# A mixture-of-experts loop on one core: one code for the first block of every expert, and a short branch that takes a second block over the same weights

## The chip, the cores and the metric

The kernel runs on one core of a Trainium2 chip. The metric is the device time of one execution in microseconds (us). The chip, the inputs and the reference are the same before and after the change. The core's engines each follow a program of their own: TensorE (PE) multiplies, VectorE (DVE) and ScalarE (ACT) do element-wise work, SyncE (SP) issues the transfers. They meet at semaphores.

## The reference, cut to what matters

Two transformer blocks over 256 tokens of width 1024. The first has a recurrent branch, an attention and a feed-forward part; the second has two attentions and a mixture of 32 experts. The change is in the experts alone:

```python
logits = (xf @ w_router + b_router).astype(jnp.float32)
top_val, top_idx = lax.top_k(logits, TOP_K)            # 4 of 32 experts for each token
gates = jax.nn.softmax(top_val, axis=-1)
...
hid = xb @ w_mlp1[e] + b_mlp1[e]                       # 1024 -> 2048
glu = jnp.minimum(hid[..., ::2], SWIGLU_LIMIT)
lin = jnp.clip(hid[..., 1::2], -SWIGLU_LIMIT, SWIGLU_LIMIT)
act = glu * jax.nn.sigmoid(SWIGLU_ALPHA * glu) * (lin + 1.0)
return act @ w_mlp2[e] + b_mlp2[e]                     # 1024 -> 1024
```

256 tokens with 4 experts each give 1024 assignments, 32 for an expert on the mean. Everything is float32. Each expert's weights are 12 MB: 8 MB for the first product (the up stage) and 4 MB for the second (the down stage).

## The kernel before, in words

The program first runs the two blocks' dense parts, written out straight. Then comes one loop over the 32 experts, written out for each position `x` from 0 to 32, inside a `While` that repeats only when an expert has more than 128 tokens (here it runs once).

**Positions.** VectorE ranks the experts by their counts. Positions 0 and 1 keep experts 0 and 1; the others are filled from the ranking, the fullest at positions 13, 19, 7, 25 and so on. The rank table is known at run time only, so SP reads the expert number of a position from `order` before it loads its weights.

**Blocks.** A block is 64 tokens of an expert (`CAP`). Every expert computes one block. An expert with more than 64 tokens (`many[x]`, read by `crowded`) computes a second block with the same weights. In this data two experts do, at positions 13 and 19.

**Weights.** SP streams them from HBM into `ring`, 17 slots of 1 MB. An expert has 12 pieces of 1 MB: 8 of the up stage, 4 of the down stage. Piece `i` may be written when piece `i - 17` has been used, which TensorE tells by `m_piece`. In the list of pieces the up pieces of position `x + 1` stand ahead of the down pieces of `x`. The first 17 of the 384 pieces are loaded before the loop starts; the other 367 are issued inside it.

**One turn of the loop on TensorE**, at position `x`: the branch on `many[x]` (L962); the up stage `up(x, blocks)` (L898 adds the bias, L909 multiplies by the weights), written twice, once for both blocks and once for the first alone; the gather of the tokens of `x + 1` (L829); at every other position `add_pair` (L944), which adds the results of two experts to the output; the branch on `many[x - 1]` (L991) around the down stage `down(x - 1, blocks, m)` (L924), again written twice, with the transposes `turns(x)` (L845, L840) among it; then `gates(x + 1)` (L835) and the branch of `second_block(x + 1)` (L866), which gathers the tokens of a second block. The untaken code lies in the program all the same: the branch jumps over it.

**The other engines.** VectorE clips and multiplies the hidden values (L2064 to L2073 for the first block, L2084 to L2093 for the second), ScalarE computes the sigmoid and copies transposed tiles back. Where an expert has no second block, each engine's `Else` raises the semaphores (`n_...`) that the second block would have raised.

Of the kernel before, what the change touches and what calls it, by code (L numbers as in the profile page):

```python
# [15 lines left out]
S = 256  # L16
# [99 lines left out]
zer f_sq f_acc f_tr  # L116
# [6 lines left out]
m_at m_aT m_ypa m_ypv m_pair m_left m_rank m_rank_v m_perm m_order  # L123
n_vec n_sel n_gath n_xg n_selt n_selT n_xet n_xe n_glu n_hid n_sig n_actd n_at n_aT n_y n_out
# [17 lines left out]
class Board:  # L142
# [244 lines left out]

    def up_at(self, x):

        return 12 * x - 4 if x else 0  # L390
# [20 lines left out]
def sync_program(e, K):  # L411
# [64 lines left out]
def tensor_program(e, K):  # L476
# [329 lines left out]
    e.wait_ge(S.zer, 1)  # L806
# [74 lines left out]
    def up(x, blocks):  # L881
        if x:
            e.wait_ge(S.m_aT, x)
            e.wait_ge(S.n_aT, x)
            e.wait_ge(S.n_y, x - 1)
        for c in blocks:
            if c:
                e.wait_ge(S.n_xe, x + 1)
                e.wait_ge(S.n_selT, x + 1)
            if c and x >= 2:  # L890
                e.wait_ge(S.m_ypa, x - 1)
                e.wait_ge(S.m_ypv, x - 1)
            if c and x == 0:
                e.wait_ge(S.m_order, 1)
            for n in range(2):
                for hf in range(2):
                    o0 = hf * 1024 + n * 512
                    mm(HID[c][n][64 * hf:64 * hf + 64, :], K.sel96[:, x:x + 1].to_broadcast([96, 64]),  # L898
                       K.b1h[:, o0:o0 + 512], start=True, stop=False, skip_group_check=True)
        for k in range(8):  # L900
            v = expert_piece(K.up_at(x) + k)
            if k == 0:
                e.wait_ge(S.m_xe, x + 1)
            xo = 128 * (k % 4) + 64 * (k // 4)
            for c in blocks:
                for n in range(2):
                    for hf in range(2):
                        o0 = hf * 1024 + n * 512
                        ins = mm(HID[c][n][64 * hf:64 * hf + 64, :], K.xe[c][x % 2][:, xo:xo + 64], v[:, o0:o0 + 512],  # L909
                                 start=False, stop=(k == 7), skip_group_check=True)  # L910
                        if k == 7 and c == n == 0 and hf == 1:
                            ins.then_inc(S.m_up0, 1)
            ins.then_inc(S.m_piece, 1)

    def down(x, blocks, m):

        v = expert_piece(K.down_at(x) + m)
        for j in range(2):
            kt = 2 * m + j
            q, hf = kt % 4, kt // 4  # L920
            for c in blocks:
                for oh in range(2):
                    g = 64 * (oh if c else oh ^ x % 2)
                    ins = mm(B[1 if c else 2][g:g + 64, :], K.aT[c][x % 2][:, 128 * q + 64 * hf:128 * q + 64 * hf + 64],  # L924
                             v[:, j * 1024 + oh * 512:j * 1024 + oh * 512 + 512], start=(kt == 0), stop=(kt == 7),
                             skip_group_check=True)
        ins.then_inc(S.m_piece, 1)
# [20 lines left out]
    with e.While(lambda: rest_of(e, K) > 0):  # L948
# [11 lines left out]
        for x in range(NE + 1):  # L960
            if x < NE:
                with e.If(many[x]):  # L962
                    up(x, (0, 1))
# [4 lines left out]
                with e.Else():  # L968
                    up(x, (0,))
# [12 lines left out]
            else:  # L982
# [5 lines left out]
                if x >= 2:  # L988
                    e.wait_ge(S.m_ypa, x - 1)
                    e.wait_ge(S.m_ypv, x - 1)  # L990
                with e.If(many[x - 1]):  # L991
                    turns(x)
                    e.wait_ge(S.n_aT, min(x + 1, NE))
                    e.wait_ge(S.m_hid, min(2 * x + 2, 2 * NE))
                    for m in range(4):
                        down(x - 1, (0, 1), m)
                    e.wait_ge(S.n_y, x)
                    e.wait_ge(S.n_selT, x)
                    for tt in range(2):
                        for oh in range(2):  # L1000
                            ins = mm(OUT[tt][oh][:, :],  # L1001
                                     K.selT[(x - 1) % 2][64 * oh:64 * oh + 64, tt * 128:(tt + 1) * 128],
                                     K.ysb[64 * oh:64 * oh + 64, :], start=False, stop=False, skip_group_check=True)
                    ins.then_inc(S.n_out, 1)
# [29 lines left out]
def scalar_program(e, K):  # L1034
# [296 lines left out]
    def second_block(x):  # L1331
        with e.If(many[x]):
            e.wait_ge(S.n_gath, x + 1)
            act(K.xg, B[3][:, :], ACT.Copy).then_inc(S.n_xg, 1)
            e.wait_ge(S.n_xet, x + 1)
            act(K.xe[1][x % 2], B[3][:, :], ACT.Copy).then_inc(S.n_xe, 1)
# [6 lines left out]
    def activate(x):  # L1343
# [7 lines left out]
        with e.If(many[x]):  # L1351
# [6 lines left out]
            if x >= 2:  # L1358
                e.wait_ge(S.m_piece, K.down_at(x - 2) + 4)
# [8 lines left out]
    with e.While(lambda: rest_of(e, K) > 0):  # L1368
# [4 lines left out]
        for x in range(NE + 1):  # L1373
# [12 lines left out]
            if x:  # L1386
                with e.If(many[x - 1]):
                    e.wait_ge(S.m_piece, K.down_at(x - 1) + 4)
# [33 lines left out]
def vector_program(e, K):  # L1422
# [499 lines left out]
    e.memset(K.zeros, 0.0).then_inc(S.zer, 1)  # L1922
# [51 lines left out]
    def ranks():  # L1974
# [3 lines left out]
        stt(key, K.cntf[0:96], 32.0, tie, ALU.mult, ALU.add).then_inc(S.m_rank_v, 1)  # L1978
        e.wait_ge(S.m_rank_v, 1)
        tt_(hit, key, rep, ALU.mult).then_inc(S.m_rank_v, 1)  # L1980
        e.wait_ge(S.m_rank_v, 2)
        e.tensor_reduce(K.rk[:, 0:1], hit, AX.X, ALU.add).then_inc(S.m_rank_v, 1)
        e.wait_ge(S.m_rank_v, 3)
        ts_(above, key, K.rk[:, 0:1], None, ALU.is_gt).then_inc(S.m_rank_v, 1)
        e.wait_ge(S.m_rank_v, 4)
        e.tensor_reduce(K.rk[:, 1:2], above, AX.X, ALU.add).then_inc(S.m_rank_v, 1)
        e.wait_ge(S.m_rank_v, 5)
# [4 lines left out]
    def in_order():  # L1992
# [3 lines left out]
        e.tensor_copy(K.order[:, 64:96], B[2][0:1, 128:160]).then_inc(S.m_rank_v, 1)  # L1996
        e.wait_ge(S.m_rank_v, 6)
# [29 lines left out]
    def second_block(x):  # L2027
# [47 lines left out]
    def second_activate(x):  # L2075
        w = K.actb[1]
        with e.If(many[x]):
# [16 lines left out]
        with e.Else():  # L2094
            if x:
                e.wait_ge(S.n_actd, 2 * x)
            e.sem_inc(S.n_glu, 2)
# [4 lines left out]
    with e.While(lambda: rest_of(e, K) > 0):  # L2102
# [31 lines left out]
        e.wait_ge(S.m_left, 1)  # L2134
# [4 lines left out]
        e.wait_ge(S.m_left, 2)  # L2139
# [113 lines left out]
```

## Time and profile before

| | us |
|---|---|
| median of three runs | 1862.34 (1857.36 to 1863.3) |
| the profiled execution, its own time | 1857.66 |
| span of its profile, first to last instruction | 1855.9 |
| TensorE busy in the span | 1674.7 (90%) |
| TensorE's weight loads | 927.6 (50%) |
| VectorE busy | 534.5 (29%) |
| ScalarE busy | 332.4 (18%) |

The profiled execution takes 1.8 us more than its span. The expert loop begins on TensorE at about 801 us and its last matmul ends at 1832 us of the span (1828.36 + 3.67); what follows (a last norm, a transpose back and the store) takes 24 us. TensorE's busy time is the union of matmuls that overlap in pairs: the two halves of its columns work side by side. Idle time that is marked "issue" is time in which the engine waited for nothing that the profile shows: no semaphore came late in it.

### The profile page before, as it was taken

To read this page: it belongs to the slowest core of one execution; us is meant where nothing else is said; L and a number is where in the kernel's file an instruction comes from. 1 tells how busy PE (TensorE), PEld (TensorE's weight loads), DVE (VectorE), ACT (ScalarE), POOL (GpSimd) and SP (SyncE) were. 2 spreads that over 40 slices of the span, in tenths; PEclk is the share of its full clock that TensorE was granted. 3 is DMA by queue.
4 is the path that set the end of the run, shared out by engine and by line. 5 is a ranking of instruction groups with operands and counts; after the bars stand their busy time and mean duration, and the time that the engine had idled before them with its cause. 6 is when DMAs were issued, how large, how long until landed. Compare 5 with 4: busy or idle time off the path is not lost. (4 is left out here: it accounts for less than half of the span.)

```text
span 1855.9 us, 20731 instructions
## 1 busy us (share of the span) xinstructions
PE 1674.7 (90%) x7662; PEld 927.6 (50%) x7662; DVE 534.5 (29%) x1309; ACT 332.4 (18%) x604; POOL 0.2 (0%) x4
## 2 busy tenths in 40 slices
PE   5999898999999888788799997989998879999785
PEld 3888776888588765533233332323333323433232
DVE  2655421766200375321111211111121111121111
ACT  2135652121100133210101110000110000111002
POOL 0000000000000000000000000000000000000000
PEclk9999999999999898979899998989998999999897
DMA  9744358335895230349999999979998789999990
GB/s 390 317 159 167 128 183 329 122 136 202 324 421 186 95 114 8 109 186 398 400 372 415 415 416 415 417 311 348 416 415 341 311 321 368 415 415 416 415 399 29
DMA packets 93340, 544.99 MB, mean 294 GB/s; under 512 B 8912, under 2 KB 9424, under 8 KB 44016
## 3 DMA queue, kind: packets, MB, share of 16 engines
q1 hardware_dynamic: 92144, 540.87, 73.1%
q8 instruction: 122, 2.00, 0.4%
q10 hardware_dynamic: 1024, 1.71, 0.3%
q14 instruction: 50, 0.41, 0.1%
HBM read 541.50 MB, written 1.05 MB: 292 GB/s over the span
## 5 line engine op out<-in xcount | busy, mean ns | idle before, releaser
L909 PE MATMUL bank<-ring,scr 128*64 128x512 f32 x2176 | 503.8, 621 | 11.4 <-issue 11.4
L491 PE MATMUL bank<-hT,ring 128*128 128x256 f32 x1856 | 414.0, 384 | 9.6 <-ACT hT L1057 7.3
L491 PEld LDWEIGHTS bank<-hT,ring 128*128 128x128 f32 x1856 | 356.4, 193 | 64.8 <-issue 13.8
L909 PEld LDWEIGHTS bank<-ring,scr 128*64 128x64 f32 x2176 | 175.3, 144 | 325.0 <-issue 321.3
L924 PE MATMUL bank<-ring,hT 128*64 128x512 f32 x1024 | 235.4, 597 | 1.3 <-DVE hT L2128 1.3
L2064 DVE TENSOR_SCALAR scr<-bank 128x256 f32<-128x256 f32 x64 | 27.0, 422 | 493.8 <-PE bank L909 493.8
L924 PEld LDWEIGHTS bank<-ring,hT 128*64 128x64 f32 x1024 | 71.7, 137 | 135.7 <-issue 135.7
L1350 ACT ACTIVATE scr<-scr 128x256 f32<-128x256 f32 x64 | 26.7, 417 | 600.1 <-DVE scr L2064 600.1
L2128 DVE COPY hT<-bank 64x512 f32<-64x512 f32 x32 | 22.2, 694 | 316.9 <-PE bank L924 316.9
L650 PE MATMUL bank<-scr,ring 128*128 128x256 f32 x384 | 83.4, 379 | 0.1
L829 PE MATMUL bank<-scr 128*64 128x512 f32 x272 | 73.1, 648 | 6.6 <-DVE scr L2036 4.6
L650 PEld LDWEIGHTS bank<-scr,ring 128*128 128x128 f32 x384 | 72.9, 190 | 10.2 <-issue 0.3
L898 PE MATMUL bank<-scr 96*64 96x512 bf16 x136 | 26.3, 474 | 52.1 <-issue 51.4
L944 PE MATMUL bank<-hT,scr 128*128 128x512 f32 x128 | 60.4, 616 | 0.8 <-ACT hT L1399 0.8
L1383 ACT ACTIVATE hT<-bank 128x512 f32<-128x512 f32 x32 | 19.1, 597 | 212.6 <-PE bank L845 212.6
L829 PEld LDWEIGHTS bank<-scr 128*64 128x64 f32 x272 | 21.7, 146 | 47.0 <-issue 39.1
L510 PE MATMUL bank<-ring,crep 128*32 128x512 f32 x384 | 42.7, 594 | 0.8 <-DMA ring<-in_w_ada 0.8
L944 PEld LDWEIGHTS bank<-hT,scr 128*128 128x128 f32 x128 | 23.7, 195 | 39.0 <-issue 37.3
L845 PEld LDWEIGHTS bank<-con,scr 128*128 128x128 f32 x136 | 15.1, 147 | 40.7 <-issue 25.0
L898 PEld LDWEIGHTS bank<-scr 96*64 96x64 bf16 x136 | 5.7, 116 | 58.9 <-issue 58.9
L499 PE MATMUL bank<-scr,con 128*128 128x256 f32 x40 | 14.8, 457 | 22.3 <-ACT scr L1078 16.3
L845 PE MATMUL bank<-con,scr 128*128 128x128 f32 x136 | 23.7, 300 | 12.1 <-DVE scr L2093 10.6
(369 smaller groups left out, 1273.4 us busy)
## 6 DMA issues: line engine op xcount, KB each, us to landing
ring<-in_w_mlp SPq DMA_DIRECT2D x384, 1024.0 KB, 14.0
ring<-in_w_in SPq DMA_DIRECT2D x28, 1024.0 KB, 25.6
ring<-in_ada_w SPq DMA_DIRECT2D x24, 1024.0 KB, 4.9
ring<-in_up SPq DMA_DIRECT2D x24, 1024.0 KB, 12.3
ring<-in_w_ada SPq DMA_DIRECT2D x24, 1024.0 KB, 9.0
ring<-in_down SPq DMA_DIRECT2D x12, 1024.0 KB, 25.9
ring<-in_w2in SPq DMA_DIRECT2D x6, 1024.0 KB, 26.9
ring<-in_w_out SPq DMA_DIRECT2D x4, 1024.0 KB, 5.8
```

The source lines that it names most:

```text
L491: ins = mm(b[:, 256 * j:256 * j + 256], v[:, k * 256 + j * 128:k * 256 + j * 128 + 128], rhs[:, k, :], start=(k == 0), stop=(k == 7))
L510: ins = mm(B[5][32 * j:32 * j + 32, :], K.crep[:, k, :], v[:, 512 * j:512 * j + 512], start=(k == 0), stop=(k == 7))
L650: ins = mm(b[j][:, 0:256], v[:, k * 256 + j * 128:k * 256 + j * 128 + 128], K.ff[:, kk * 8 + k, :], start=(kk == 0 and k == 0), stop=(kk = ...
L829: ins = mm(B[3][64 * hf:64 * hf + 64, :], K.sel[c][:, tt, :], K.h4[:, tt, hf * 512:(hf + 1) * 512], start=(tt == 0), stop=(tt == 1), skip_ ...
L845: ins = e.transpose(B[c][:, 128 * q:128 * q + 128], K.actb[c][:, 128 * q:128 * q + 128], ident)
L898: mm(HID[c][n][64 * hf:64 * hf + 64, :], K.sel96[:, x:x + 1].to_broadcast([96, 64]), K.b1h[:, o0:o0 + 512], start=True, stop=False, skip_g ...
L909: ins = mm(HID[c][n][64 * hf:64 * hf + 64, :], K.xe[c][x % 2][:, xo:xo + 64], v[:, o0:o0 + 512], start=False, stop=(k == 7), skip_group_ch ...
L924: ins = mm(B[1 if c else 2][g:g + 64, :], K.aT[c][x % 2][:, 128 * q + 64 * hf:128 * q + 64 * hf + 64], v[:, j * 1024 + oh * 512:j * 1024 + ...
L944: ins = mm(OUT[tt][oh][:, :], K.pairT[p % 2][oh][:, tt * 128:(tt + 1) * 128], K.ypair[oh], start=False, stop=False, skip_group_check=True)
L1350: act(K.w2[:, sl], K.actb[0][:, sl], ACT.Sigmoid, scale=1.702).then_inc(S.m_sig, 1)
L2064: ts_(w[:, sl], gate, 7.0, None, ALU.min).then_inc(S.m_glu, 1)
L2128: e.tensor_copy(K.ypair[1 - (x - 1) % 2][64:128, :], B[2][64:128, :]).then_inc(S.m_ypv, 1)
```

## The change

The second block gets code of its own, on TensorE alone:

- `up(x)` now computes the first block of every expert and stands ahead of the branch. The branch on `many[x]` then holds `second_up(x)`, which passes over the same 8 pieces again.
- In the down stage the pieces of the first block (`down(x - 1, m)`), with `turns(x)` ahead of the last one as it was for uncrowded experts, stand ahead of the branch. The branch holds `second_down(x - 1)`, which passes over the same 4 pieces again and adds the second block to the output.
- `m_piece` is now raised when the first block has used a piece. Two new semaphores, `n_up` and `n_down`, count the second uses. Before SP overwrites a piece it waits for both. Where there is no second block, VectorE's `Else` raises `n_up` by 8 (in `second_block`) and `n_down` by 4 (in `second_activate`).
- The waits of ScalarE and VectorE that meant "both blocks have used this" now name `n_up` or `n_down`. Three semaphores are folded into others (`zer` into `consts`, `m_rank_v` into `m_left`), with the same waits.

```diff
+    def second_use(self, i):
+
+        if i < 8:
+            return self.S.n_up, i + 1
+        x, n = (i - 8) // 12, (i - 8) % 12
+        if x < NE - 1 and n < 8:
+            return self.S.n_up, 8 * (x + 1) + n + 1
+        return (self.S.n_down, 4 * x + n - 7) if x < NE - 1 else (self.S.n_down, 4 * x + n + 1)
...
             e.wait_ge(S.m_piece, i - RING + 1)
+            second, value = K.second_use(i - RING)
+            e.wait_ge(second, value)
             src = K.moe_source(i, expert[x])
...
+    def second_up(x):
+
+        e.wait_ge(S.n_xe, x + 1)
+        e.wait_ge(S.n_selT, x + 1)
+        if x >= 2:
+            e.wait_ge(S.m_ypa, x - 1)
+            e.wait_ge(S.m_ypv, x - 1)
+        if x == 0:
+            e.wait_ge(S.m_order, 1)
+        up_bias(x, 1)
+        for k in range(8):
+            v = expert_piece(K.up_at(x) + k)
+            xo = 128 * (k % 4) + 64 * (k // 4)
+            for n in range(2):
+                for hf in range(2):
+                    o0 = hf * 1024 + n * 512
+                    ins = mm(HID[1][n][64 * hf:64 * hf + 64, :], K.xe[1][x % 2][:, xo:xo + 64], v[:, o0:o0 + 512],
+                             start=False, stop=(k == 7), skip_group_check=True)
+            ins.then_inc(S.n_up, 1)
...
+    def second_down(x):
+
+        e.wait_ge(S.n_aT, min(x + 2, NE))
+        e.wait_ge(S.m_hid, min(2 * x + 4, 2 * NE))
+        for m in range(4):
+            down_piece(x, 1, m).then_inc(S.n_down, 1)
+        e.wait_ge(S.n_y, x + 1)
+        e.wait_ge(S.n_selT, x + 1)
...
             if x < NE:
+                up(x)
                 with e.If(many[x]):
-                    up(x, (0, 1))
+                    second_up(x)
                     e.wait_ge(S.n_actd, 2 * x + 2)
                     e.wait_ge(S.n_hid, 2 * x + 2)
                     e.wait_ge(S.m_hid, 2 * x + 2)
                     turn_hidden(1).then_inc(S.n_at, 1)
                 with e.Else():
-                    up(x, (0,))
                     if x:
                         e.wait_ge(S.n_at, x)
                     e.sem_inc(S.n_at, 1)
...
+                for m in range(3):
+                    down(x - 1, m)
+                turns(x)
+                down(x - 1, 3)
                 with e.If(many[x - 1]):
-                    turns(x)
-                    e.wait_ge(S.n_aT, min(x + 1, NE))
-                    e.wait_ge(S.m_hid, min(2 * x + 2, 2 * NE))
-                    for m in range(4):
-                        down(x - 1, (0, 1), m)
...
+                    second_down(x - 1)
                 with e.Else():
-                    for m in range(3):
-                        down(x - 1, (0,), m)
-                    turns(x)
-                    down(x - 1, (0,), 3)
...
             if x:
                 e.wait_ge(S.n_selT, x)
+                e.wait_ge(S.n_up, 8 * x)
+            e.sem_inc(S.n_up, 8)
...
-                e.wait_ge(S.m_piece, K.up_at(x) + 8)
+                e.wait_ge(S.n_up, 8 * x + 8)
...
             if x:
                 e.wait_ge(S.n_actd, 2 * x)
+                e.wait_ge(S.n_down, 4 * x)
+            e.sem_inc(S.n_down, 4)
```

**The up stage in TensorE's program.** In the program before, this stands at each position from `x = 2` on, where a turn of the loop begins (one row may be several matmuls, `x64` for instance; a float32 matmul of these rows becomes two records of a matmul and two of a weight load in the profile, a bfloat16 one or a transpose one of each):

```order
L962 COMPARE_AND_BRANCH
L898 MATMUL bank<-scr 64x512 x8
L909 MATMUL bank<-ring,scr 64x512 x64
L845 MATMUL bank<-con,scr 128x128 x4
L962 UNCONDITIONAL_BRANCH
L898 MATMUL bank<-scr 64x512 x4
L909 MATMUL bank<-ring,scr 64x512 x32
L968 UNCONDITIONAL_BRANCH
L829 MATMUL bank<-scr 64x512 x4
```

In the changed program the same place reads:

```order
L896 MATMUL bank<-scr 64x512 x4
L913 MATMUL bank<-ring,scr 64x512 x32
L1003 COMPARE_AND_BRANCH
L896 MATMUL bank<-scr 64x512 x4
L935 MATMUL bank<-ring,scr 64x512 x32
L856 MATMUL bank<-con,scr 128x128 x4
L1003 UNCONDITIONAL_BRANCH
L1009 UNCONDITIONAL_BRANCH
L840 MATMUL bank<-scr 64x512 x4
```

The branch has moved from ahead of the up stage to behind it, and it now skips one pass of 32 weight matmuls where it skipped 64.

**The down stage in TensorE's program.** Before, the end of the skipped code, the code for one block, and what follows it:

```order
L1001 MATMUL bank<-scr 128x512 x4
L991 UNCONDITIONAL_BRANCH
L924 MATMUL bank<-ring,hT 64x512 x12
L845 MATMUL bank<-con,scr 128x128 x4
L840 MATMUL bank<-con,scr 128x128 x4
L924 MATMUL bank<-ring,hT 64x512 x4
L1005 UNCONDITIONAL_BRANCH
L835 MATMUL bank<-con,scr 128x128 x2
L866 COMPARE_AND_BRANCH
```

In the changed program, from the first down piece on:

```order
L946 MATMUL bank<-ring,hT 64x512 x12
L856 MATMUL bank<-con,scr 128x128 x4
L851 MATMUL bank<-con,scr 128x128 x4
L946 MATMUL bank<-ring,hT 64x512 x4
L1035 COMPARE_AND_BRANCH
L946 MATMUL bank<-ring,scr 64x512 x16
L965 MATMUL bank<-scr 128x512 x4
L1035 UNCONDITIONAL_BRANCH
L1037 UNCONDITIONAL_BRANCH
L846 MATMUL bank<-con,scr 128x128 x2
L877 COMPARE_AND_BRANCH
```

The branch of the down stage now comes behind the last piece and skips 16 weight matmuls and 4 that add to the output; two branches (L1035 and L877) stand close together ahead of the next up stage.

## Rows read from the trace of the kernel before

**Rows 1.** The page: span; GB/s in 40 slices of the span.
```profile
span 1855.9 us, 20731 instructions
GB/s 390 317 159 167 128 183 329 122 136 202 324 421 186 95 114 8 109 186 398 400 372 415 415 416 415 417 311 348 416 415 341 311 321 368 415 415 416 415 399 29
```

**Rows 2.** The chain that ended last, positions 26 to 28: start, us, what.
```profile
1641.16 0.55 PE bank L898 x4
1641.71 13.73 PE bank L909 x64
...
1665.57 0.55 PE bank L898 x4
...
1693.77 0.55 PE bank L898 x4
```

**Rows 3.** SP's transfers from 806 us; two stretches: PEclk, DMA share, GB/s last.
```profile
806.51 42.60 SPq L444 DMA_DIRECT2D ring<-in_w_mlp  x17
829.00:834.00 5.00, 5.00 (x18) 1.80 (x16) 0.93 (x4) 0.00 (x0) 0.00 (x0) 0.58 0.02 7
1600.00:1700.00 100.00, 100.00 (x466) 36.80 (x464) 21.66 (x60) 12.43 (x24) 0.00 (x0) 1.00 1.02 415
```

**Rows 4.** TensorE's waits, positions 2 to 30: us in total, times, longest.
```profile
PE bank L898 <- issue: 50.6, 10, 5.5
PE bank L909 <- issue: 6.4, 3, 2.6
```

**Rows 5.** TensorE's timeline at positions 11, 20 and 29; idle ahead in brackets.
```profile
1120.22 1.07 PE L898 MATMUL bank<-scr 96*64 96x512 bf16 x4 [4.66 <-issue]
...
1453.61 1.06 PE L898 MATMUL bank<-scr 96*64 96x512 bf16 x4 [4.69 <-issue]
...
1723.33 1.06 PE L898 MATMUL bank<-scr 96*64 96x512 bf16 x4 [5.14 <-issue]
```

**Rows 6.** The chain that ended last, positions 22 and 23.
```profile
1524.75 5.47 issue
...
1531.29 16.29 PE bank L909 x64
...
1561.26 1.90 issue
```

**Rows 7.** TensorE's timeline at the loop's end.
```profile
1791.95 15.80 PE L909 MATMUL bank<-ring,scr 128*64 128x512 f32 x64 [4.98 <-issue]
...
1825.63 1.89 PE L924 MATMUL bank<-ring,hT 128*64 128x512 f32 x8
...
1828.36 3.67 PE L944 MATMUL bank<-hT,scr 128*128 128x512 f32 x8 [0.84 <-ACT hT L1399]
```

**Rows 8.** The page's third part: packets, MB, share of the program queue.
```profile
q8 instruction: 122, 2.00, 0.4%
```

**Rows 9.** TensorE in stretches, the ten up stages behind waits: clock third from last.
```profile
1530.20:1547.40 17.20, 17.18 (x69) 0.82 0.73 282
...
sum 165.50, PE 165.27; mean PE 16.53
```

**Rows 10.** The page's groups: count, busy, mean ns, idle before them and its releaser.
```profile
L909 PE MATMUL bank<-ring,scr 128*64 128x512 f32 x2176 | 503.8, 621 | 11.4 <-issue 11.4
L924 PE MATMUL bank<-ring,hT 128*64 128x512 f32 x1024 | 235.4, 597 | 1.3 <-DVE hT L2128 1.3
```

**Rows 11.** Timelines of positions 13 (first row) and 19, on TensorE and VectorE.
```profile
1190.98 1.47 PE L898 MATMUL bank<-scr 96*64 96x512 bf16 x8
...
1397.10 28.99 PE L909 MATMUL bank<-ring,scr 128*64 128x512 f32 x128
1431.38 0.90 PE L845 MATMUL bank<-con,scr 128*128 128x128 f32 x3 [5.29 <-DVE scr L2093]
...
1428.17 0.42 DVE L2084 TENSOR_SCALAR scr<-bank 128x256 f32<-128x256 f32 x1
...
1430.57 0.75 DVE L2093 TENSOR_TENSOR scr<-scr 128x256 f32<-128x256 f32 x2
```

More of the change, by code:

```diff
@@ L879, in second_block, with up_bias, up @@
             e.sem_inc(S.n_selt, 1)
-    def up(x, blocks):
+    def up_bias(x, c):
+        for n in range(2):
+            for hf in range(2):
+                o0 = hf * 1024 + n * 512
+                mm(HID[c][n][64 * hf:64 * hf + 64, :], K.sel96[:, x:x + 1].to_broadcast([96, 64]),
+                   K.b1h[:, o0:o0 + 512], start=True, stop=False, skip_group_check=True)
+    def up(x):
         if x:
@@ L885, in up @@
             e.wait_ge(S.n_y, x - 1)
[L886 to L899, printed above, removed]
+        up_bias(x, 0)
         for k in range(8):
@@ L904, in up, with down_piece @@
             xo = 128 * (k % 4) + 64 * (k // 4)
[L905 to L912, printed above, removed]
-            ins.then_inc(S.m_piece, 1)
-    def down(x, blocks, m):
+            for n in range(2):
+                for hf in range(2):
+                    o0 = hf * 1024 + n * 512
+                    ins = mm(HID[0][n][64 * hf:64 * hf + 64, :], K.xe[0][x % 2][:, xo:xo + 64], v[:, o0:o0 + 512],
+                             start=False, stop=(k == 7), skip_group_check=True)
+                    if k == 7 and n == 0 and hf == 1:
+                        ins.then_inc(S.m_up0, 1)
+            ins.then_inc(S.m_piece, 1)
+    def second_up(x):
[10 more added lines that the diff above has]
+            xo = 128 * (k % 4) + 64 * (k // 4)
+            for n in range(2):
+                for hf in range(2):
+                    o0 = hf * 1024 + n * 512
+                    ins = mm(HID[1][n][64 * hf:64 * hf + 64, :], K.xe[1][x % 2][:, xo:xo + 64], v[:, o0:o0 + 512],
+                             start=False, stop=(k == 7), skip_group_check=True)
+            ins.then_inc(S.n_up, 1)
+    def down_piece(x, c, m):
         v = expert_piece(K.down_at(x) + m)
@@ L920, in down @@
             q, hf = kt % 4, kt // 4
[L921 to L927, printed above, removed]
+            for oh in range(2):
+                g = 64 * (oh if c else oh ^ x % 2)
+                ins = mm(B[1 if c else 2][g:g + 64, :], K.aT[c][x % 2][:, 128 * q + 64 * hf:128 * q + 64 * hf + 64],
+                         v[:, j * 1024 + oh * 512:j * 1024 + oh * 512 + 512], start=(kt == 0), stop=(kt == 7),
+                         skip_group_check=True)
+        return ins
+    def down(x, m):
+        down_piece(x, 0, m).then_inc(S.m_piece, 1)
+    def second_down(x):
[5 more added lines that the diff above has]
+        e.wait_ge(S.n_selT, x + 1)
+        for tt in range(2):
+            for oh in range(2):
+                ins = mm(OUT[tt][oh][:, :], K.selT[x % 2][64 * oh:64 * oh + 64, tt * 128:(tt + 1) * 128],
+                         K.ysb[64 * oh:64 * oh + 64, :], start=False, stop=False, skip_group_check=True)
+        ins.then_inc(S.n_out, 1)
     def turns(x):
@@ L1977, in ranks @@
         rep, tie, at = K.rankc[:, 0:32], K.rankc[:, 32:64], K.rankc[:, 64:96]
[L1978 to L1987, printed above, removed]
+        stt(key, K.cntf[0:96], 32.0, tie, ALU.mult, ALU.add).then_inc(S.m_left, 1)
+        e.wait_ge(S.m_left, 1)
+        tt_(hit, key, rep, ALU.mult).then_inc(S.m_left, 1)
+        e.wait_ge(S.m_left, 2)
+        e.tensor_reduce(K.rk[:, 0:1], hit, AX.X, ALU.add).then_inc(S.m_left, 1)
+        e.wait_ge(S.m_left, 3)
+        ts_(above, key, K.rk[:, 0:1], None, ALU.is_gt).then_inc(S.m_left, 1)
+        e.wait_ge(S.m_left, 4)
+        e.tensor_reduce(K.rk[:, 1:2], above, AX.X, ALU.add).then_inc(S.m_left, 1)
+        e.wait_ge(S.m_left, 5)
         ts_(K.sel96, at, K.rk[:, 1:2], None, ALU.is_equal)
@@ L1995, in in_order @@
         e.tensor_copy(K.gpx.rearrange("p a b -> p (a b)"), B[2][:, 0:128])
-        e.tensor_copy(K.order[:, 64:96], B[2][0:1, 128:160]).then_inc(S.m_rank_v, 1)
-        e.wait_ge(S.m_rank_v, 6)
+        e.tensor_copy(K.order[:, 64:96], B[2][0:1, 128:160]).then_inc(S.m_left, 1)
+        e.wait_ge(S.m_left, 6)
         e.tensor_single_scalar(K.order[:, 0:32], K.order[:, 64:96], 31, ALU.bitwise_and)
```

28 lines of the change are left out of this document (11 added, 17 removed).

## The prediction

> **What bounds the kernel now.** I read the page first, then the chain that ended last, then TensorE's waits and timeline. More than half of the span is the expert loop, from 801 to 1832 us. The page's slices of it show 415 GB/s in many places, and 311 to 372 in seven [rows 1].
>
> Two things run against each other there. TensorE needs 24.4 and 28.2 us for two quiet positions (from the bias at 1641.16 to the next at 1665.57, and on to 1693.77 [rows 2]), 26.3 on the mean. The weights of a position are 12 pieces of 1.049 MB; at the 415 GB/s of a full stretch [rows 3] a piece takes 2.53 us and a position 30.3. So the loads are the slower of the two and should never stop. They do stop: TensorE falls behind somewhere, and its ring of 17 fills.
>
> The waits tell where. Ahead of the bias of an up stage (L898) TensorE is idle ten times, 50.6 us in all, with no semaphore late [rows 4]. Counted along the timeline, it is at positions 2, 3, 4, then 11, 12, then 20, 21, 22, then 29, 30; the rows show 11, 20 and 29 [rows 5]. Three positions wait a shorter time inside the up stage (6.4 us in all [rows 4], as the 1.90 at 1561 [rows 6]), and the last position 4.98 [rows 7]. The pattern has a period of nine positions, whatever the data. What else repeats with the position is the program: each turn has about the same number of instructions, so after nine turns it stands again at the same phase of the unit in which the program is fetched. And the place is always right behind the branch of L962, which jumps over the code for two blocks. I therefore read these waits as TensorE's code: the jump's target hasn't been fetched. Code comes in pieces of 2.00 MB / 122 = 16.4 KB [rows 8].
>
> Behind each full wait the granted clock is low for a while: 0.82 of full speed over the up stage of position 22 [rows 9], which is full speed (2.4 GHz) and some us at the lower level (1.2); TensorE had been idle 5.47 us before [rows 6]. The ten up stages take 165.5 us from bias to gather [rows 9]; an undisturbed one takes 0.55 + 13.73 = 14.28 [rows 2]. The low clock costs 165.5 - 142.8 = 22.7 us.
>
> **The code that is skipped.** The order rows give 64 weight matmuls in the code that L962 jumps over. The count of records (2176 for 34 blocks of 32 matmuls [rows 10]) says two matmul records each, and as many weight loads: 256 instructions. With 8 bias matmuls and 4 transposes at 2 each it is 280, and some 287 with waits and branches. After the change it is 128 + 8 + 8 and the like, some 149. In the down stage it was 32 weight matmuls, 4 that add up and 8 transposes, some 164 instructions; now it is 16 and 4, some 84. The price of shorter skips stands in the trace: L991 passes over its 164 instructions 30 times, and the down stage's matmuls never wait for issue, only 1.3 us for VectorE [rows 10]. So 164 is free, 287 costs about 5 us in a third of its cases, and 149 and 84 lie below the free one. I take zero for both; the bound from the other side is that 149 costs in proportion to its length, half of today's waits.
>
> The Trainium skill ("Runtime: NRT & Kernel Launch", "Instruction fetch mechanics") says that code is refilled in blocks of 16 KiB, 256 instructions, strictly in sequence, and that a taken branch to a target outside the current two blocks stalls. The trace agrees with the block's size. By that rule a skip of 287 can pass a whole block and one of 149 or 84 can't: the zero above. But the same section gives TensorE room for 2048 instructions; by that figure a skip of 287 would hardly miss, the waits would be something else, and the time would be that of the no-change rival below.
>
> **The sum on TensorE.**
> - Ten waits ahead of the bias: -50.6.
> - Four shorter ones: -6.4 - 4.98 = -11.4. I take them as the same fetch seen later: the jump landed near the end of a unit, and the next was still coming.
> - The low clock behind the ten: -22.7. Behind the last position's wait: 15.80 [rows 7] less some 13.9 (the chain's 13.73 [rows 2] and the last record's tail), -1.9.
> - Positions 13 and 19. The up stage has the same matmuls, 128 records in 28.99 us [rows 11]. Then TensorE waited 5.29 us for VectorE, whose chain for the second block ran from 1428.17 to 1431.32, 3.15 us, behind the first block's. Now the first block's lies beside the 14 us of the second pass, and 3.3 us remain: -2.0 each, -4.0.
> - The branches at their new places. The one on `many[x]` (L1003) now comes behind 32 weight matmuls that TensorE still works off: 0. L1035 stands behind the last down piece, with L877 shortly behind; before, L866 and L962 stood there: 0. The bound above is 0.1 us in each of 32 turns, 3 us.
> - SP's added waits are on counts that VectorE raises well before; at one piece in 2.53 us nothing is late behind them: 0.
>
> That is -90.6, and TensorE would end its loop at 1832.0 - 90.6 = 1741.4.
>
> **The sum on the loads.** The first of the 367 is issued at 806.51 [rows 3], when position 0 has used a piece; nothing can be earlier, as the ring is full until then. Near 829 to 834 us nothing moves (7 GB/s [rows 3]), in a part before any of the waits: +4.4. Then 367 x 2.527 = 927.3. The last piece lands at about 806.5 + 4.4 + 927.3 + 2 (my estimate for the way of one piece) = 1740.2. Behind it lie its eight matmuls 1.89, 0.84 for copying and the last pair 3.67 [rows 7]: 6.4. The loop can't end before 1746.6.
>
> **Which is last.** Position 13 starts at 1190.98 [rows 11]; half of 50.6 + 22.7 and a short wait of 2 fall away ahead of it, so TensorE is there at about 1152. Its first piece is the 136th of the loop's loads: 806.5 + 4.4 + 343.7 + 2 = 1156.6. The 17 pieces of lead are used up by then and TensorE waits some 5 us; the second block then gives the loads their lead back. TensorE's sum becomes 1746, beside 1746.6. Two limits that meet cost a little more than either; I take 1748, 84 us earlier than now. What follows the loop is untouched. The profiled execution's own 1857.66 becomes 1773.6, and 1775 with half of the branches' bound. The median of the runs shown, 1862.3, is 4.7 above the profiled one; I add one: **1776**.
>
> What is late next is the load stream: at positions 9 to 12 and at the end TensorE should stand idle for pieces.
>
> **The rivals.**
> - *Half of the waits stay*, because 149 misses in proportion: five waits of 5.06 + 2.27, 37 us, so 1813. Against it: 164 never missed.
> - *The ring is held.* At positions 13 and 19 eight pieces stay for a second pass of 14.3 us and four for 7.2. If all loads stopped that long, 2 x 21.5 = 43 us: 1819. Against it: 17 - 8 = 9 slots hold 22.7 us of loads, more than 14.3, as long as TensorE isn't many pieces behind when it comes there; by the sum it is ahead. I take 0, the bound is 43.
> - *No change.* The idle isn't code but a semaphore raised late by an `Else`, which the profile doesn't name. Then only -4.0: 1854. Against it: the period of nine.
> - *Slower.* It is not the length but two jumps in a row that make code late: today's ten waits stand behind L866 and L962, and L1035 and L877 are such a pair in every turn. A wait costs 5.06 + 2.27 = 7.3 us; from 90.6 / 7.3 = 12.4 such positions on the kernel is slower, at 30 it is at 1857.7 - 90.6 + 219 = 1986. Against it: the same pair passes twenty positions without a wait today, and the new pair skips only 115 instructions together.
> - *The clock.* Starved of pieces, TensorE may be granted the lower level where it wasn't; an up piece then takes 3.43 instead of 13.73 / 8 = 1.72 us, more than its load. If that happens in a third of some 60 starved us the loop loses about ten: 1786. It widens the range.
>
> **How the numbers follow.** Forecast 0.72, at 1766 to 1795; half stays 0.12; ring held 0.05; no change 0.04; slower 0.03; other mixtures between, 0.04. The range 1764 to 1806 holds the forecast with its bounds (clock, branches, load rate) and the lower part of the second case: 8 in 10. Faster by over 0.3% (about what a measurement of this kernel can tell from no change) 0.94, within 0.3% 0.03, slower 0.03.
>
> **What the profile after would show.** Right: no issue wait ahead of the bias (L896); under 100 packets in the program's queue; slices of the loop near 415 GB/s except the first; TensorE idle ahead of the up stage's weight matmuls (L913), short and often, at positions 9 to 12 and the end; 3.3 us of waiting at 13 and 19. Wrong: waits of about 5 us behind L1003 or L877 at every n-th position (code is still late), or none and yet under 400 GB/s around positions 13 and 19 (the ring is held). With the mechanism right, the load rate would make the number wrong: one per cent of it is 9 us.

## The result, and the profile after

The changed kernel takes 1789.03 us (median of four, 1787.89 to 1797.2) beside 1861.86 of the kernel before on the same chip: 0.962 of its time, 95% interval 0.960 to 0.965. The forecast was 1776, with a range of 1764 to 1806. A second timing of the same kernel (`again`, below) gave the same ratio, 0.962. The profiled execution was the slowest of the four, at 1797.2.

The page of the changed kernel:

```profile
span 1795.4 us, 21192 instructions
...
GB/s 394 336 141 174 131 131 392 109 120 220 218 422 312 115 120 47 71 50 327 417 415 417 416 417 416 416 417 413 415 415 362 367 379 418 415 418 414 418 415 123
...
q8 instruction: 95, 1.56, 0.4%
...
L913 PE MATMUL bank<-ring,scr 128*64 128x512 f32 x2048 | 458.4, 599 | 20.3 <-DMA ring<-in_w_mlp 20.0
...
L946 PE MATMUL bank<-ring,hT 128*64 128x512 f32 x1024 | 234.1, 597 | 4.4 <-DMA ring<-in_w_mlp 3.3
```

Of the seven slices of the loop that had stood at 311 to 372 GB/s [rows 1], three are left, 362, 367 and 379. The program queue moves 95 packets for 122 [rows 8]. TensorE's waits in the loop (us in total, times, longest):

```profile
PE bank L913 <- DMA ring<-in_w_mlp: 20.0, 36, 1.4
PE bank L856 <- DVE scr L2125: 6.7, 2, 3.4
PE bank L840 <- DVE scr L2066: 4.6, 2, 2.3
PE bank L946 <- DMA ring<-in_w_mlp: 3.3, 6, 0.6
...
PE bank L896 <- issue: 0.2, 1, 0.2
```

The 50.6 us ahead of the bias [rows 4] are 0.2. In their place TensorE waits 36 times ahead of the up stage's weight matmuls and 6 times ahead of the down stage's, all for pieces, 23.3 us. L856 are the transposes of the second block's hidden values at the crowded positions 13 and 19: 3.35 us of waiting each where it had been 5.29 [rows 11].

The records of the branches themselves, on TensorE's sequencer, show what the waits only suggest. Columns: count, duration of one in ns (shortest, median, longest). The kernel before:

```profile
L962 PEldq COMPARE_BRANCH  x34: 70/345/6071, 802.0 to 1785.6; - x34
L991 PEldq COMPARE_BRANCH  x34: 70/333/4421, 843.2 to 1820.0; - x34
```

and after:

```profile
L1003 PEldq COMPARE_BRANCH  x34: 70/208/346, 818.7 to 1744.2; - x34
L1035 PEldq COMPARE_BRANCH  x34: 70/210/369, 854.8 to 1764.5; - x34
```

In the kernel before, L962 takes 5.2 to 6.1 us at exactly the ten positions of the waits, and under 0.6 at all others; afterwards no branch takes over 0.4. The row of L991 also corrects a reading of mine: one of its 34 did take 4.42 us (at 1228, in the turn of position 13), behind matmuls that TensorE had still to work off, so that no wait was to be seen. A skip of 164 was nearly free, not free. That one record stands 1.2 us behind another jump: TensorE had just left the code for two blocks and passed over the up stage for one.

What is left is in the loads. The timeline of position 19, and stretches around it and behind it (granted clock third from last, GB/s last):

```profile
1369.50 1.06 PE L896 MATMUL bank<-scr 96*64 96x512 bf16 x4
1370.35 15.86 PE L913 MATMUL bank<-ring,scr 128*64 128x512 f32 x64
1386.04 0.60 PE L896 MATMUL bank<-scr 96*64 96x512 bf16 x4
1386.48 13.90 PE L935 MATMUL bank<-ring,scr 128*64 128x512 f32 x64
```
```profile
1370.00:1380.00 10.00, 10.00 (x40) 3.12 (x38) 0.86 (x5) 0.00 (x0) 0.00 (x0) 0.79 1.02 421
1380.00:1384.00 4.00, 4.00 (x22) 1.34 (x20) 0.00 (x0) 0.00 (x0) 0.00 (x0) 1.00 0.73 307
1384.00:1388.00 4.00, 4.00 (x24) 1.36 (x22) 2.29 (x7) 0.83 (x2) 0.00 (x0) 1.00 0.31 127
1388.00:1392.00 4.00, 4.00 (x20) 1.24 (x18) 0.66 (x2) 0.00 (x0) 0.00 (x0) 1.00 0.54 197
...
1412.00:1425.00 13.00, 13.00 (x68) 4.75 (x66) 2.47 (x7) 1.68 (x3) 0.00 (x0) 1.00 0.78 297
```
```profile
1346.00:1481.00 135.00, 127.28 (x566) 43.30 (x564) 23.39 (x66) 14.96 (x29) 0.00 (x0) 0.95 0.92 369
1482.00:1650.00 168.00, 168.00 (x784) 57.84 (x785) 34.93 (x97) 19.21 (x37) 0.00 (x0) 1.00 1.02 416
```

While the first pass (L913) runs, SP may not overwrite any of the eight pieces: it issues nothing between 1366.3 and 1388.6, the seven pieces that are on their way when the pass begins land, and the rate falls from 421 to 127 GB/s. The second pass (L935) then sets the pieces free one by one. A smaller hole follows at the down pieces (297). From 1482 on the loads run at 416 again, and nothing of what was lost comes back, since they are the bound.

The stream of loads, from the first issue in the loop to the last landing, takes 953.2 us here (811.17 to 1764.39), against 367 x 2.527 = 927.3 at the full rate; `again` has 947.5. The rest of the text uses this length for every kernel. The kernel before has 1005.4.

### The profile page after: what moved, and what is told of

It is laid out like the page before. It is cut to its first block and busy times, and to the rows that moved or that the text cites. A ratio compares the mean times of both kernels' runs of the same rounds, so it can differ in the third digit from the quotient of the medians.

```text
span 1795.4 us, 21192 instructions
## 1 busy us (share of the span) xinstructions
PE 1658.9 (92%) x7662; PEld 902.5 (50%) x7662; DVE 534.1 (30%) x1309; ACT 332.6 (19%) x604; POOL 0.2 (0%) x4
## 5 line engine op out<-in xcount | busy, mean ns | idle before, releaser
L913 PE MATMUL bank<-ring,scr 128*64 128x512 f32 x2048 | 458.4, 599 | 20.3 <-DMA ring<-in_w_mlp 20.0
L502 PEld LDWEIGHTS bank<-hT,ring 128*128 128x128 f32 x1856 | 360.1, 195 | 65.6 <-issue 14.2
L913 PEld LDWEIGHTS bank<-ring,scr 128*64 128x64 f32 x2048 | 142.4, 138 | 318.9 <-issue 255.1
L661 PEld LDWEIGHTS bank<-scr,ring 128*128 128x128 f32 x384 | 72.9, 190 | 10.2 <-issue 0.3
L1768 DVE TENSOR_SCALAR scr<-scr,col 128x256 f32<-128x256 f32 x48 | 19.7, 410 | 51.4 <-ACT scr L1234 51.3
L856 PEld LDWEIGHTS bank<-con,scr 128*128 128x128 f32 x136 | 14.9, 145 | 34.7 <-issue 26.2
L1234 ACT ACTIVATE scr<-bank 128x512 f32<-128x512 f32 x24 | 14.4, 599 | 96.7 <-PE bank L502 96.6
L2054 DVE COPY scr<-bank 64x256 f32<-64x256 f32 x64 | 27.0, 423 | 12.7 <-PE bank L846 11.4
```

Of the source, the lines that this page charges most:

```text
L502: ins = mm(b[:, 256 * j:256 * j + 256], v[:, k * 256 + j * 128:k * 256 + j * 128 + 128], rhs[:, k, :], start=(k == 0), stop=(k == 7))
L661: ins = mm(b[j][:, 0:256], v[:, k * 256 + j * 128:k * 256 + j * 128 + 128], K.ff[:, kk * 8 + k, :], start=(kk == 0 and k == 0), stop=(kk = ...
L913: ins = mm(HID[0][n][64 * hf:64 * hf + 64, :], K.xe[0][x % 2][:, xo:xo + 64], v[:, o0:o0 + 512], start=False, stop=(k == 7), skip_group_ch ...
L2054: ins = e.tensor_copy(K.pairT[x // 2 % 2][g ^ x % 2][rows, :], B[3][rows, 0:256])
```

## The experiments

Twelve runs followed, one of them the changed kernel once more. Each is given by its ratio to the kernel before, timed beside it on the same chip.

### What makes code late: the length of the skip

**skip218** and **skip279** put no work into the branch, only instructions to pass over: waits on a count that was reached long ago. They lengthen the skip of L1003 from 149 to 218 and to 279 instructions.

```diff
                 with e.If(many[x]):
+                    for _ in range(138):
+                        e.wait_ge(S.pos, 1)
                     second_up(x)
```

(138 become 69 instructions; skip279 has 260, which become 130.)

> The changed kernel with 69 more instructions (waits on a semaphore that is long up) in the branch on many[x] behind the up stage, so that an uncrowded position jumps over 218 instead of 149. Theory (the program is fetched in units of 256 instructions, one unit ahead; a jump waits only if it passes a whole unit or lands just short of the next): no issue wait at any position, time 1789 to 1797 (the two crowded positions execute the 69 waits, some 3.5 us each). Rival (waits in proportion to the length of the skip): 0.76 of the ten waits of before, 7 or 8 of them at 5 us, time near 1830.

> The same with 130 more instructions, a skip of 279. Theory: full issue waits of 4.5 to 6 us behind the up stage's branch at positions 7, 9, 16, 18, 27 and 29, shorter ones (1 to 5 us, inside the gather and what follows) at 5, 14 and 25, again a pattern with a period of about nine, worked out from where the jumps stand in the program; time 1825 to 1840, as a part of the loss lies in time in which TensorE waits for pieces. Rival (the wait comes from a late semaphore, or from having two jumps close together): no such waits, time as skip218.

Measured: skip218 1802.11, ratio 0.970 (0.966 to 0.973); skip279 1827.27, ratio 0.981 (0.976 to 0.986). The branch's records in both, skip218 first:

```profile
L1003 PEldq COMPARE_BRANCH  x34: 70/330/451, 813.5 to 1746.4; - x34
```
```profile
L1003 PEldq COMPARE_BRANCH  x34: 70/344/6122, 817.0 to 1773.1; - x34
```

At 218 no branch is late. At 279 the branch is late at positions 7, 9, 16, 18, 27 and 29, the six forecast, by 1.0 to 6.1 us. The shorter waits forecast at 5, 14 and 25 are there too (1.4, 0.5 and 1.0 us). The jump ahead of this one lies 11 us or more back in all six cases, so the skip of 279 is late by itself. That settles length as a cause. TensorE's waits in skip279:

```profile
PE bank L896 <- issue: 20.0, 2, 10.1
PE bank L913 <- DMA ring<-in_w_mlp: 10.7, 21, 0.6
PE bank L840 <- PEq L1014: 10.6, 4, 4.6
```

Of some 6 us of a late branch only 10.6 / 4 = 2.7 us on the mean are idle time (2.0 at three of the four positions and 4.6 at one), because the branch now stands behind 32 weight matmuls that TensorE still has in its queue. The 20.0 us are the price of the padding itself: at 13 and 19 TensorE walks through it, 10 us each, with eight pieces held all the while (240 GB/s over 1390 to 1440). skip218 pays 7.6 us in the same way, its stream takes 960.5, and its time is 5 us above the range it was given. So neither kernel's total prices a skip; the branch's records do.

### One part alone

**up_only** keeps the new up stage and does the down stage as before, both blocks in the branch, one block in the `Else`:

```diff
-                for m in range(3):
-                    down(x - 1, m)
-                turns(x)
-                down(x - 1, 3)
                 with e.If(many[x - 1]):
+                    turns(x)
                     second_down(x - 1)
                 with e.Else():
+                    for m in range(3):
+                        down(x - 1, m)
+                    turns(x)
+                    down(x - 1, 3)
```

(`second_down` there does both blocks of each piece, as `down(x - 1, (0, 1), m)` did before.) **down_only** is the reverse, the new down stage with the up stage of before:

```diff
-                up(x)
                 with e.If(many[x]):
-                    second_up(x)
+                    both_up(x)
...
                 with e.Else():
+                    up(x)
```

> Only the up stage is changed; the down stage of both blocks stands in the branch on many[x - 1] as before (skip 164, up stage's skip 149). Theory: all issue waits are gone with the up stage's change alone; time within 5 us of the changed kernel, 1784 to 1794, and the down pieces of positions 13 and 19 are given back one by one, so a little less hold on the ring. Rival (the down stage's shorter skip shares the gain): 1805 to 1825.

> Only the down stage is changed; the up stage is again written twice behind a branch that skips 287 instructions. Theory: issue waits ahead of the bias are back, at other positions since each turn of the program is shorter: full ones at 2, 4, 9, 11, 16, 18, 23, 25 and 30, shorter ones at 14, 21 and 28; time 1843 to 1860. Rival (both skips matter alike): near 1825.

Measured: up_only 1794.5, ratio 0.966 (0.962 to 0.970); down_only 1888.64, ratio 1.017 (1.013 to 1.021), slower than before. The expectation of down_only was a miss, in sign; up_only ended half a us above its range, and its rival is out. The waits of down_only, and the records of its branch at the old place:

```profile
PE bank L896 <- issue: 69.9, 17, 5.6
PE bank L913 <- issue: 12.6, 5, 3.8
```
```profile
L1013 PEldq COMPARE_BRANCH  x34: 70/437/6178, 807.0 to 1819.6; - x34
```

The up stage's branch skips 287 instructions as before, and yet it is late at 16 of 30 positions instead of 10. What has changed is the code ahead of it: the branch of the down stage, which used to stand 4 pieces earlier, now stands behind the last piece and skips 84; the branch of the next block skips 31; then come 287. That is 402 instructions passed over within 2.5 us, in three jumps. In the kernel before it was 31 + 287 = 318.

So what counts is not one jump but what is passed over in a row. The count that this suggests, late at (skipped - 256) / 256 of the positions, with the 256 from the packets (below), against the thirty positions of each kernel:

| kernel | passed over in a row | by this count | long records of the branch |
|---|---|---|---|
| after | 84 + 31 = 115, or 149 | 0 | 0 |
| skip218 | 218 | 0 | 0 |
| skip279 | 279 | 2.7 | 6 |
| up_only | 149 + 164 = 313 | 6.7 | 8 |
| before | 31 + 287 = 318 | 7.3 | 10 |
| down_only | 84 + 31 + 287 = 402 | 17.1 | 16 |

It gets the order and the zeros right and is up to 3.3 off. It was made after these runs, so I take it for a rule of thumb.

up_only shows the other half. Its branch behind the down stage (L1047, 164) is now late at eight positions:

```profile
L1047 PEldq COMPARE_BRANCH  x34: 70/330/4533, 841.0 to 1748.3; - x34
```
```profile
PE bank L913 <- DMA ring<-in_w_mlp: 17.4, 33, 0.6
...
PE bank L946 <- issue: 1.8, 2, 1.5
```

and hardly anyone waits for it, 1.8 us in all: 2.6 to 4.5 us of lateness lie behind the queued matmuls.

These eight records also show how jumps add up. The up stage's jump ends 1.3 to 3.2 us before each of them, and the shorter that distance, the longer the record: 1.33 and 4.53 us, 2.14 and 3.71, 3.21 and 2.75. In all eight the two add up to 5.7 to 6.0 us, about the length of a late record that stands alone. The one long record of L991 in the kernel before fits (1.24 + 4.42 = 5.7), and so do the eight records of 3.3 to 3.8 us in down_only, counted from the end of the down stage's jump (5.5 to 6.0). So I read it as one fetch that the first jump starts and whose rest the next jump waits for.

The interval of up_only overlaps with the full change's (0.960 to 0.965). The new up stage alone brings the gain, as far as these timings can tell; the new down stage isn't needed for it, and alone it does harm.

### What the loads cost

**light_after** and **light_before** load half of each piece in the loop, so the results leave out half of the expert weights; TensorE's work is the same.

```diff
+                src, dst = src[:, :, 0:512], dst[:, :, 0:512]
...
+                src, dst = src[:, 0:1024], dst[:, 0:1024]
```

> The changed kernel with half-size weight loads inside the expert loop (0.5 MB instead of 1 MB for each of the 367 pieces; the other half of a slot keeps old data, so the experts' results leave out half of the weights; the work on every engine is the same). Theory: with the loads out of the way TensorE's own sum shows. The trace of the changed kernel has 23.3 us of waits for pieces, so about 1766 (1760 to 1770), which is also the 1767 of the prediction's sum on TensorE. Rival (the loads aren't what ends last, TensorE is): within 5 us of 1789.

> The same halving in the kernel before. Theory: TensorE never waits for a piece there, so 1857 to 1863, the same as before, and its issue waits stay ten plus four. Rival (the issue waits are made long by the load traffic through which the program is fetched): waits clearly under 5 us each, and a time 15 us or more below 1860.

Measured: light_after 1757.49, ratio 0.947 (0.945 to 0.948); light_before 1825.36, ratio 0.982 (0.978 to 0.986). In light_after no wait for a piece is left. The changed kernel is bound by its loads, and with half of their bytes it gains (0.9623 - 0.9465) x 1860, some 29 us, of which 23.3 are the waits for pieces. That is 2.5 us below the range of the expectation.

light_before was expected at no change and is 32 us faster, as its rival had it. Its waits:

```profile
PE bank L903 <- issue: 36.7, 10, 4.3
...
PE bank L914 <- issue: 3.6, 3, 2.8
```

There are still ten, at 3.67 us instead of 5.06, and the branch's records there are 3.5 to 5.0 us long instead of 5.2 to 6.1. Fetching code takes longer while the full weights stream than with half of their bytes. The shorter waits are 13.9 us ahead of the bias and, with the last position's, 11.4 - 3.6 = 7.8 inside the up stage, 21.7 of the 33.2 us between the two profiled executions. The other 11.5 are about what TensorE's busy time is shorter (1663.0 for 1674.7), at a mean granted clock of 0.957 for 0.951.

### Holding the ring

**halves** shortens the time for which pieces are held: four up pieces, the second block's pass over them, then the other four.

```diff
-                up(x)
+                up(x, 0)
+                with e.If(many[x]):
+                    second_up(x, 0)
+                up(x, 1)
                 with e.If(many[x]):
-                    second_up(x)
+                    second_up(x, 1)
```

**place9** moves the crowded expert of position 13 to position 9 (every expert's weights are loaded and used as before, only the order differs); **place15** moves the one of position 19 to 15, so that the two stand close together.

```diff
-PLACES = [13, 19, 7, 25, 16, 10, 22, 4, 28]
+PLACES = [9, 19, 7, 25, 16, 10, 22, 4, 28]
```

(In place15 the list begins with 13, 15.)

> The changed kernel with the second pass of the up stage in two halves: after pieces 0 to 3 a branch takes the second block over them, after 4 to 7 another. At most four pieces are held. Theory (the ring, held at position 19, stops the loads for some 15 us): the stop behind 1370 us falls from about 10 us to none, the one in the down stage stays; time 1777 to 1784. Rival (the loads lost there are made up later, or other waits set the end): 1786 to 1792.

> The changed kernel with the fullest expert at position 9 instead of 13 (the tables of places alone). TensorE is starved of pieces from about 8 on, so the second block there costs nothing, and ten quiet positions, 40 us of catching up, lie ahead of position 19 instead of six. Theory: no stop of the loads at either position, loads end 12 to 20 us earlier; time 1770 to 1778. Rival (hold doesn't matter): 1786 to 1792.

> The changed kernel with its two fullest experts at positions 13 and 15 instead of 13 and 19 (the tables of places alone). TensorE comes to 15 some 11 to 14 pieces behind the loads, so that almost nothing is outstanding when it holds eight. Theory (the hold costs load time, and load time ends last): the loads stop for 25 to 40 us about position 15, time 1797 to 1815. Rival (the hold is harmless): within 4 us of the changed kernel.

> The changed kernel once more, beside the next three on the same chip: 1786 to 1792. Its loads in the loop take about 950 us from the first issue to the last landing, of which 15 are lost behind position 19, where the ring is held.

| kernel | median us | ratio to before, 95% | stream of loads us |
|---|---|---|---|
| after | 1789.03 | 0.9623 (0.9595 to 0.9652) | 953.2 |
| again | 1790.61 | 0.9622 (0.9599 to 0.9645) | 947.5 |
| halves | 1789.81 | 0.9639 (0.9621 to 0.9656) | 948.1 |
| place9 | 1782.70 | 0.9600 (0.9583 to 0.9618) | 940.4 |
| place15 | 1802.57 | 0.9689 (0.9668 to 0.9711) | 963.6 |

`again` and place15 lie in their ranges. place9 is 5 us above its range: it gains 7.1 us of stream where 12 to 20 were expected, though its rival (no gain) is out as well.

The stretch of position 19 in place9, then in `again`:

```profile
1346.00:1481.00 135.00, 129.55 (x592) 43.93 (x588) 23.39 (x66) 13.88 (x27) 0.00 (x0) 0.98 1.01 413
```
```profile
1346.00:1481.00 135.00, 127.26 (x580) 43.55 (x578) 22.92 (x65) 14.11 (x27) 0.00 (x0) 0.97 0.97 386
```

and in place15 its first pass at position 15, and the stretch around it:

```profile
1256.00:1273.00 17.00, 17.00 (x84) 5.61 (x82) 2.94 (x8) 0.83 (x2) 0.00 (x0) 1.00 0.17 55
```
```profile
1180.00:1330.00 150.00, 139.27 (x636) 47.39 (x634) 25.84 (x73) 16.39 (x32) 0.00 (x0) 0.98 0.88 355
```

The place of the crowded positions decides. The starts of positions 13 and 19 in `again`, on TensorE:

```profile
1164.65 0.62 PE L896 MATMUL bank<-scr 96*64 96x512 bf16 x4
...
1360.42 0.62 PE L896 MATMUL bank<-scr 96*64 96x512 bf16 x4
```

These six positions take 195.8 us, where six quiet ones take 6 x 26.3 = 157.8: a crowded position costs TensorE 38 us more than a quiet one, and a quiet one brings back 30.3 - 26.3 = 4. By that 38 / 4, nine to ten positions, are needed until it has caught up with the loads; in place9 it waits for pieces again in the eighth position behind the crowded one (at 1292). Six apart (13 and 19) it comes to the second one still behind; ten apart (9 and 19) the loads run through at 413 GB/s; two apart (13 and 15) they all but stop, at 55 GB/s for 17 us. The loads of six positions take 6 x 30.3 = 181.8 us, so in `again` TensorE comes to the second crowded position 14.0 us further behind than to the first; in place15 it is 88.5 (1165.85 to 1254.34) - 60.6 = 27.9, another 13.9. From place9 to `again` the profiled streams differ by 7.1 us and the spans (1776.5 and 1784.0) by 7.5; from `again` to place15 by 16.1 and (1784.0 and 1800.2) by 16.2. The same microseconds that the loads lose the kernel loses.

halves missed its expectation. SP's pause at the up pieces of position 19 is down to 10.2 us from the 17.0 of `again`, but its stream is as long. The loads are lost one stage later, at the down pieces, in `again` (first row) as in halves (second):

```profile
1400.00:1412.00 12.00, 12.00 (x62) 4.40 (x62) 2.47 (x7) 1.68 (x3) 0.00 (x0) 1.00 0.76 272
```
```profile
1400.00:1412.00 12.00, 12.00 (x55) 4.48 (x56) 0.74 (x2) 1.68 (x4) 0.00 (x0) 1.00 0.65 231
```

In `again` the pause of 17.0 us costs the stream nothing: nine pieces are on their way when it begins, and a piece lands every 2.5 us until 1401.5, though the rate dips to 344 GB/s over 1370 to 1384. The next lands only at 1407.0. SP had given out its eight slots by 1389.2 and had to wait until 1402.0, when TensorE, behind the second pass, the gather and `add_pair`, had used the first down piece; that is a plain first use, no held one. The second uses alone don't cost the loads either: at position 13 the same eight pieces are held, and the page after shows 413 to 417 GB/s around it. up_only, which gives the down pieces back one by one, has a stream of 949.2 us. So what costs is how far TensorE is behind when a crowded position makes it later still, with only 17 slots between it and the loads; how long single pieces are held matters little beside it. Only in the profiled execution shown above, where TensorE was later (seven pieces on their way at 1370.35, its pass 15.86 us for 13.90 at a lower clock), did the hold itself open a hole: nothing landed between 1387.5 and 1393.4.

### Put together

**place9_up** is place9 with up_only's down stage, **place9_halves** place9 with halves.

> The fullest expert at position 9, and the down stage of both blocks piece by piece inside its branch, as before the change: the least hold that doesn't lengthen the up stage's skip. Theory: loads at full rate throughout, time 1776 to 1784, at or 2 us under place9. Rival (the longer skip of the down branch, 164 behind 149, costs code waits that show once TensorE has no lead): 1786 to 1795.

> The fullest expert at position 9, and the second up pass in halves. Theory: as place9, 1776 to 1784, since place9 alone has already no full stop of the loads.

Measured: place9_up 1781.02, ratio 0.958 (0.956 to 0.960), and place9_halves 1781.41, ratio 0.957 (0.955 to 0.959). Their streams are 941.1 and 940.3, as in place9. Both lie in their ranges, and ahead of `again` (0.962, 0.960 to 0.965), timed beside them, by (0.962 - 0.9575) x 1860, some 8 us, though place9_up's interval just touches it. Between themselves and from place9 nothing can be told. These are the fastest versions that ran.

## Why the prediction was right, and where it was short

**The cause, the ten waits, the skips.** Right. The branch's records put the ten waits on the jump, and skip279 brings late branches back at the positions counted out beforehand. The 27 packets fewer stand for 30792 - 23872 = 6920 instructions fewer in TensorE's program, 256 each: the unit that the argument rested on. "164 is free" was right only for that place: one of its records was 4.42 us long and hidden, and in up_only the same 164, close behind another jump, is late at eight positions.

**The crowded positions, -4.0.** 3.35 us instead of 5.29, twice: -3.9.

**Branches and SP's waits at 0.** Right: no branch takes over 0.37 us, and no issue wait is left but 0.2.

**What is last.** Right: the loads, with TensorE starved ahead of L913 from about position 8 to 12 and at the end, 23.3 us.

**The size.** 13 us short, nearly all on the sum of the loads. It had 4.4 + 927.3 + 2 = 933.7 us of stream; `again` has 947.5, 13.8 more, and begins it 1.4 us earlier (805.1 for 806.5): 12.4 us, and its own 1785.8 is 10.8 to 12.2 above the 1773.6 to 1775 of the forecast. The medians are 13 and 15 above 1776, a little more, because I added one us from the profiled execution to the median; it had been 4.7 in the kernel before and is 4.8 in `again`. (The profiled execution shown above is 11.4 longer than this one: it began the stream at 811.2, 6.0 later, and took 5.7 longer over it.)

The step that failed is "the ring is held: I take 0", by its premise "by the sum it is ahead". I had worked out TensorE's state for 13 alone, and had put the second block at 14.3 + 7.2 us and a short wait where it costs 38. So at 19 it is behind: in `again` eight pieces lie landed and unused and nine are on their way. The argument that nine slots outlast 14.3 us came true there, but it looked at the up pieces only; the loads stop at the down pieces behind them. Of the bound of 43 us, place9, where only four pieces lie landed when TensorE comes to 19, gets 7.1 back in the stream.

place9 still has 6.7 over 933.7. Some 3.3 of them are code: between 801 and 1750 us it moves 386.20 MB, of which 1.35 are instructions, and the 415 GB/s of the sum count both. Another 1.7 lie in the first dozen pieces, which take 36.4 us for 30.3 where I had 4.4 us of stop. The last 1.7 I can't place.

That 1789 lies in the range is in part luck: the range was made wide for the clock, the branches and the load rate, and what filled it was mainly a stop of the loads that I had put at nothing.

**The clock rival.** It didn't happen. (By its own numbers, 20 pieces of 3.43 us for 2.53, it would have cost 18 us and not ten.) Where TensorE is starved most, it is granted the full 2.4 GHz:

```profile
1060.00:1136.00 76.00, 69.72 (x306) 22.49 (x304) 13.78 (x38) 8.74 (x17) 0.00 (x0) 1.00 1.02 416
1670.00:1760.00 90.00, 79.64 (x344) 25.01 (x346) 14.38 (x39) 8.24 (x16) 0.00 (x0) 1.00 1.01 412
```

**TensorE's own sum.** It gave 1767, and light_after took 1757.5 without waiting for a piece: so the sum is at most 10 us too high (14 by the profiled execution, 1753.2). It can't be read as exact, since light_before shows that with half the bytes code comes sooner too. It wasn't the bound, so nothing followed from it.

**The slower rival.** Its mechanism is real, though it was given 0.03: jumps in a row make code late. It was ruled out for this kernel by the right count, 115 instructions together, and down_only is the kernel in which it decides. It isn't a rival to length, though, since the lengths add up.

## What to carry to other kernels

When an engine idles with no semaphore late, look at how long its branch records are and count the instructions that it passes over in a row, over all jumps within a few us, not in one: a long body behind a branch is better made a short one that stands behind queued work. When the fix makes a stream of loads the bound, work out at every place that takes the consumer longer than its loads how far behind it already is when it comes there, not only at the first, and set such places as far apart as it takes to catch up, here ten positions and not six. Giving single buffers back sooner didn't help here.

## What the chip showed that I had not expected

- A late jump costs 5.2 to 6.1 us in the branch's record with weights streaming at 415 GB/s. With half of their bytes it costs 3.5 to 5.0.
- TensorE's queue hides a good part of it: of about 6 us behind 32 weight matmuls 2.7 are seen on the mean, and of 2.6 to 4.5 us in up_only nearly nothing.
- Jumps add up: 84 + 31 + 287 instructions within 2.5 us made 16 of 30 positions late, where 31 + 287 made 10 and 84 + 31 none. Where the first of two jumps has started the fetch, the second waits 5.5 to 6.0 us less the time since the first.
